# Keys and values of the memory between the steps of differential attention and gated memory, a choice from 100 pairs, 32 early keys, and other links around the routing

## The reference

```python
s_top, i_top = lax.top_k(s, K)                                     # K = 16, s: 128 keys
cand = s_top[:, :, 0, :, None] + s_top[:, :, 1, None, :]           # 256 sums per head
best, pos = lax.top_k(cand.reshape(T, PEER_HEADS, K * K), K)
...
a = jax.nn.gelu(jnp.einsum('thkd,td->thk', u, xb))                 # u = expert_u[ib]
out = jnp.einsum('thk,thkd->td', gb * a, expert_v[ib])
...
x = x + hybrid_mixer(rms_norm_2(x, norm_mix_g[l]), ...)            # differential attention, mLSTM
x = x + cross_attention(rms_norm_2(x, norm_x_g[l]), rms_norm_2(mem, norm_mem_g[l]), ...)
...
k = (mem_n @ wk); v = (mem_n @ wv)                                 # mem_n: 256 x 1024
```

## Time and profile before

| | us |
|---|---|
| median of 3 runs | 3126.39 |
| lowest, highest | 3126.13, 3129.74 |
| the profiled execution, its own time | 3126.0 |
| its span, first to last instruction | 3124.3 |
| busy: PE, DVE, ACT, POOL | 2733.4, 2077.2, 1336.7, 742.3 |
| mean granted clock of PE, share of 2.4 GHz | 0.935 |

### The profile page before, as it was taken

One profiled execution on the slowest core, in us unless ns is written; L12 is line 12 of the kernel. 1 busy time (PEld: TensorE's weight loads), 2 busy tenths in 40 slices (PEclk: granted clock), 3 DMA queues, 4 the chain that ended last, 5 costly groups with the idle time before them and its releaser, 6 DMA issues. The chain is left out here.

```text
span 3124.3 us, 35863 instructions
## 1 busy us (share of the span) xinstructions
PE 2733.4 (87%) x12788; PEld 2212.3 (71%) x12788; DVE 2077.2 (66%) x3565; ACT 1336.7 (43%) x2049; POOL 742.3 (24%) x562
## 2 busy tenths in 40 slices
PE   4976879799969999999999995895589699999994
PEld 3434668566757999999999994663367588888883
DVE  4334547799957777777777775415633489989984
ACT  2112552115643333333333334225333278878873
POOL 1000023141023333334334331430121221122220
PEclk8978989899989999999999997997789799999997
DMA  7710011333579988888888872220022399999993
GB/s 251 242 58 17 1 56 58 115 118 126 211 284 315 312 288 289 288 288 288 300 295 291 298 248 61 83 80 32 2 82 62 148 319 394 374 374 372 365 361 129
DMA packets 261487, 646.34 MB, mean 207 GB/s; under 512 B 47836, under 2 KB 104924, under 8 KB 260060
## 3 DMA queue, kind: packets, MB, share of 16 engines
q1 hardware_dynamic: 214892, 501.88, 44.8%
q0 software_dynamic: 46448, 142.67, 13.8%
HBM read 614.47 MB, written 55.12 MB: 214 GB/s over the span
## 5 line engine op out<-in xcount | busy, mean ns | idle before, releaser
L2826 ACT ACTIVATE ex_w_hi<-expert_raw 128x1024 fp32r<-128x1024 f32 x384 | 376.9, 1074 | 49.4 <-DMA expert_raw<-in_w 26.8
L1710 PE MATMUL bank<-v_hi,peer_w_hi 128*128 128x512 f32 x768 | 301.1, 392 | 21.5 <-DVE peer_w_lo L1816 21.5
L212 POOL TENSOR_TENSOR w_lo<-ring,w_hi 128x512 fp32r<-128x512 f32 (+1 forms) x136 | 173.3, 1306 | 557.3 <-ACT w_hi L202 557.3
L2872 DVE TENSOR_TENSOR ex_w_lo<-expert_raw,ex_w_hi 128x1024 fp32r<-128x1024 f32 x256 | 296.7, 1219 | 9.5 <-ACT ex_w_hi L2826 8.0
L1710 PE MATMUL bank<-v_hi,peer_w_lo 128*128 128x512 f32 x768 | 301.3, 392 | 0.0
L1710 PE MATMUL bank<-v_lo,peer_w_hi 128*128 128x512 f32 x768 | 301.2, 392 | 0.0
L1752 ACT ACTIVATE v_hi<-v_in 128x1024 fp32r<-128x1024 f32 x128 | 129.7, 1054 | 349.1 <-PE bank L1710 327.6
L1698 PE MATMUL bank<-h_hi,u_lo 128*128 128x384 f32 x832 | 278.6, 335 | 0.0
L1698 PE MATMUL bank<-h_hi,u_hi 128*128 128x384 f32 x832 | 278.5, 335 | 0.0
L1698 PE MATMUL bank<-h_lo,u_hi 128*128 128x384 f32 x832 | 278.3, 334 | 0.0
L1685 POOL DMA_INDIRECT got_rows<-in_u_rows,diff x128 | 186.2, 1455 | 311.9 <-DVE got_rows L1784 283.7
(11 more groups left out here) (495 smaller groups left out, 6201.2 us busy)
## 6 DMA issues: line engine op xcount, KB each, us to landing
expert_raw<-in_w SPq DMA_DIRECT2D x384, 512.0 KB, 9.2
v_in<-in_expert_v SPq DMA_DIRECT2D x128, 512.0 KB
u_in<-in_u_tiles SPq DMA_DIRECT2D x104, 512.0 KB
ada_in<-in_w_ada SPq DMA_DIRECT2D x48, 512.0 KB, 5.2
gates_by_key<-spread SPq DMA_DIRECT2D x6, 4096.0 KB, 11.5
gate_in<-gates_by_key SPq DMA_DIRECT2D x384, 64.0 KB
ring<-in_w_in SPq DMA_DIRECT2D x11, 2048.0 KB, 8.4
early_u<-in_u_tiles SPq DMA_DIRECT2D x24, 512.0 KB, 3.8
```

The source lines that it names most:

```text
L212: eng.tensor_tensor(g.w_lo[:, k, 0:cols], g.ring[u % RING][:, k, 0:cols], g.w_hi[:, k, 0:cols].bitcast(F32), ALU.subtract).then_inc(s["z_f ...
L1710: last = pe.matmul(g.bank[2 + o][:, :], x[:, par, e, i * P:(i + 1) * P], v[:, par, e, c], start=(first and n == 0), stop=(final and n == 3 ...
L2826: act.activation(hi[kind][:, c, :], raw_piece(raw, u * PIECES + c), ACT.Copy).then_inc(s["r_hi"], 1)
L2872: dve.tensor_tensor(lo[which][:, c, :], raw_piece(raw, u * PIECES + c), hi[which][:, c, :].bitcast(F32), ALU.subtract).then_inc(s["r_lo"], 1)
```

## The change

1. **Memory.** Class `MemoryRows` keeps normalising and turning in `choose_experts` and stores the result `mem_t` (1 MB) in DRAM. A new class `Memory` makes keys and values in 16 groups of 256 columns. A group is made in two halves, `part`, of four 128x256 matmuls each, in one bank (7); the next group's first part waits until ACT has copied the bank out. Ten parts stand in `differential`, one after each unit from u = 6; four stand at the head of PE's queue in `mlstm`, and 18 between its score products. Sums in `differential` then use one bank instead of two, so that each waits for ACT's copy of the one before. The weight units of the memory (19 to 22) come between those of `w_in_2` and `w_out_2`, and the loads ahead are moved with them.
2. **Choice.** `top16` runs over 100 sums instead of 256 (the 3 best first keys with all 16 second ones, the other 13 with 4). POOL adds 384 + 416 elements per token tile instead of 2048; DVE has one cast and four small operations more for the ranks.
3. **Early keys.** `EARLY_CHOOSING` is 20 instead of 12, so EQ is 16 instead of 12 and HALFWAY 38 instead of 36; after it a step gathers 128/26 = 4.92 rows. The statistics of the memory go on ACT's queue behind the second gelu instead of the fourth.
4. **Routing.** SP clears `lists` ahead of the 12 loads; the first two row gathers are issued by POOL inside `route`, as soon as `first_slots` is there; the wait for the last scatter goes from POOL's end of `run_experts` to SP in `finish`; the clearing of `moe_rows` goes into the guarded part of `run_overflow`; and the gain of `finish` is loaded first.

```diff
-EARLY_BEFORE, EARLY_CHOOSING, EARLY_SPREADING = 4, 12, 12
+EARLY_BEFORE, EARLY_CHOOSING, EARLY_SPREADING = 4, 20, 12
...
+    def part(self, pe, index):
+        j, half = index // 2, index % 2
+        n = self.groups[j]
+        u = self.first_unit + n // self.PER_UNIT
+        if half == 0:
+            g.weights(pe, u)
+            if j:
+                pe.wait_ge(s["q_out"], j)
+        w = g.ring[u % RING]
+        for k in range(half * self.HALF_K, (half + 1) * self.HALF_K):
+            ...
+            last = pe.matmul(self.slot(), x, y, start=(k == 0), stop=(k == DC - 1))
+        if half == 1:
+            last.then_inc(g.dense, 1)
...
@@ choose_experts
+LONG, SHORT = 3, 4
+PAIRS = LONG * TOPK + (TOPK - LONG) * SHORT
-                        top16(dve, count, s["h_dve"], [(sums[:, i % 2, h + j].rearrange("p a b -> p (a b)"), work[:, j, :],
+                        top16(dve, count, s["h_dve"], [(pairs[i % 2][:, h + j], work[:, j, :],
-                step(dve.tensor_scalar(rank_i[:, 1], place[:], 15, None, ALU.bitwise_and))
+                step(dve.tensor_scalar(rank_i[:, 1], place[:], 2, None, ALU.arith_shift_right))
                 step(dve.tensor_copy(rank[:], rank_i[:]))
+                step(dve.tensor_copy(place_f[:], place[:]))
+                step(dve.scalar_tensor_tensor(rank[:, 0], rank[:, 1], float(LONG - LONG * TOPK // SHORT), rank[:, 0], ALU.add, ALU.max))
+                step(dve.tensor_scalar(base[:], rank[:, 0], float(SHORT), float(LONG * (TOPK - SHORT)), ALU.mult, ALU.add))
+                step(dve.scalar_tensor_tensor(base[:], rank[:, 0], float(TOPK), base[:], ALU.mult, ALU.min))
+                step(dve.tensor_tensor(rank[:, 1], place_f[:], base[:], ALU.subtract))
@@ differential, PE
-                    if u >= 2:
-                        pe.wait_ge(s["m_y"], u - 1)
+                    if u:
+                        pe.wait_ge(s["m_y"], u)
+                    if u >= N - 2 * MEMORY_FIRST:
+                        mem.part(pe, u - (N - 2 * MEMORY_FIRST))
@@ mlstm, PE
+            BEFORE = 4
+            def parts_done(n):
+                return BEFORE + (PARTS - BEFORE) * (n + 1) // (ML_H * TT)
+                for index in range(BEFORE):
+                    mem.part(pe, index)
...
                         pe.matmul(g.bank[2 + n % 2][:, 0:T - j * P], kt[:, h, j * P:(j + 1) * P], qt[:, h, j * P:T], start=True, stop=True).then_inc(s["n_s"], 1)
+                        if j < TT - 1:
+                            for index in range(parts_done(n - 1), parts_done(n)):
+                                mem.part(pe, index)
@@ route
             def _(sp):
+                sp.wait_ge(s["q_zero"], 1)
+                sp.dma_start(table.rearrange("(r p) o -> r (p o)", p=P), zero[:, :]).then_inc(s["q_clear"], 16)
                 sp.wait_ge(g.rows_stored, 2 * TT * 16)
                 begin(sp)
-                sp.wait_ge(s["q_zero"], 1)
-                sp.dma_start(table.rearrange("(r p) o -> r (p o)", p=P), zero[:, :]).then_inc(s["q_clear"], 16)
                 sp.wait_ge(s["q_clear"], 16)
...
+                pool.wait_ge(g.rows_stored, 2 * TT * 16)
+                pool.wait_ge(s["q_first"], 1)
+                for n in range(2):
+                    gather_rows(pool, g, first_slots, x_rows, x_in, n)
@@ run_experts, POOL
-                for n in range(3):
-                    gather(n)
+                gather(2)
...
-                for par in range(2):
-                    pool.wait_ge(s[f"r_st{par}"], NE // 2 * 16)
@@ finish, SP
+                for par in range(2):
+                    sp.wait_ge(y_stored[par], NE // 2 * 16)
```

More of the change, by code:

```diff
@@ L1414, in _ @@
                 memory.sp_rows(sp)
-                for n in range(2, EARLY_BEFORE):
-                    early.load(sp, n)
-                    early.keep(sp, n - 2)
-                for n in range(EARLY_BEFORE, EARLY_BEFORE + 2):
-                    early.load(sp, n)
-                    early.keep(sp, n - 2)
-                memory.sp(sp)
-                for n in range(EARLY_BEFORE, EARLY_CHOOSING):
+                for n in range(EARLY_CHOOSING):
                     early.keep(sp, n)
@@ L1479, in _ @@
             def _(act):
-                for n in range(EARLY_BEFORE):
+                early.gelu(act, 0)
+                early.gelu(act, 1)
+                memory.act_stats(act)
+                for n in range(2, EARLY_BEFORE):
                     early.gelu(act, n)
                 memory.act(act)
-                act.wait_ge(s["h_shift"], 1)
-                act.activation(gate[:], gate[:], ACT.Exp).then_inc(s["h_exp"], 1)
                 for n in range(EARLY_BEFORE, EARLY_CHOOSING):
+                    if n == EARLY_CHOOSING // 2:
+                        act.wait_ge(s["h_shift"], 1)
+                        act.activation(gate[:], gate[:], ACT.Exp).then_inc(s["h_exp"], 1)
                     early.gelu(act, n)
@@ L1963, in _, with differential @@
                 dve.sem_inc(s["l_rot"], 1)
-def differential(g, tok):
+def differential(g, tok, memory, t, mem_t):
     nc, a = g.nc, g.a
@@ L1986, in differential @@
         ms, rms, rs = (sb(n, [P, TT * DA_H]) for n in ("da_ms", "da_rms", "da_rs"))
-        with stage(nc, "m_par m_dve m_lam m_lexp flipped flip_out m_s0 m_s1 m_max m_e0 m_e1 m_a m_t m_pt m_o m_y m_sq m_root m_gain") as (block, s):
+        with stage(nc, "m_par m_dve m_lam m_lexp flipped flip_out m_s0 m_s1 m_max m_e0 m_e1 m_a m_t m_pt m_o m_y m_sq m_root m_gain" + Memory.SEMS) as (block, s):
+            mem = memory(s, list(range(MEMORY_FIRST)))
             @block.sync
@@ L2282, in sums @@
                         pe.wait_ge(s["n_y"], 2 * (h - 1))
[L2283 to L2284 removed]
+                    for tiles in ((0, 1, 2), (3,)):
+                        if h and tiles == (3,):
+                            pe.wait_ge(s["n_y"], 2 * h)
+                        for i in tiles:
                             for j in range(i + 1):
[L2286 to L2287 removed]
+                                last = pe.matmul(sums_at(h, i, i + 1), sd[:, h % 2, j, (i - j) * P:(i - j + 1) * P], mv[:, j, h, :], start=(j == 0), stop=(j == i))
                         last.then_inc(s["n_o"], 1)
@@ L2377, with gather_rows, route @@
 RAW = 3
-def route(g, begin, table, slot, weight, first_slots, over):
+def gather_rows(pool, g, first_slots, x_rows, x_in, n):
+    rows = g.ht[:, 0:4, :].rearrange("p (b k) t -> p b (k t)", b=2)
+    pool.indirect_dma_start(out=rows[:, n % 2, :], out_offset=None, in_=x_rows,
+                            in_offset=bass.IndirectOffsetOnAxis(ap=first_slots[:, n:n + 1], axis=0),
+                            bounds_check=2 * T - 1, oob_is_err=False).then_inc(x_in[n % 2], 16)
+def route(g, begin, table, slot, weight, first_slots, over, x_rows, x_in):
     nc = g.nc
@@ L2940, in gather @@
         def gather(pool):
+            for par in range(2):
+                pool.wait_ge(y_stored[par], NE // 2 * 16)
+            pool.memset(m.rows[:, :, :], 0.0).then_inc(s["r_zero"], 1)
+            pool.wait_ge(s["r_zero"], 1)
             pool.sem_inc(s["r_go"], 1)
@@ L2992, in _, with finish @@
             guarded(dve, gates)
-def finish(g, weight, y_rows, out):
+def finish(g, weight, y_rows, out, y_stored):
     nc, a = g.nc, g.a
@@ L3084, in plan_weights @@
     g.plan(a["w_in_2"][0], W2_GATES, 2 * ML_H, 2)
+    for name in ("w_xk_2", "w_xv_2"):
+        for i in range(2):
+            g.plan(a[name][0], i * BANK, BANK, Memory.PER_UNIT)
     for i in range(2):
@@ L3105, in second_mixer, with memory @@
             project_second(g, tok, mv, conv, mi, mf, first_unit)
-            differential(g, tok)
-            mlstm(g, tok, mv, conv, mi, mf)
+            with ExitStack() as both:
+                t = both.enter_context(nc.sbuf_tensor("mem_in", [P, DC, MEM], F32))
+                piece = both.enter_context(nc.sbuf_tensor("mem_piece", [P, 2, MEM], F32))
+                def memory(s, groups):
+                    return Memory(g, s, t, piece, first_unit + 8, mem_kt, mem_v, groups)
+                differential(g, tok, memory, t, mem_t)
+                mlstm(g, tok, mv, conv, mi, mf, memory)
         def mixed(k):
```

201 lines of the change are left out of this document (122 added, 79 removed).

## The result

| | us |
|---|---|
| changed kernel, median of 6 runs (lowest, highest) | 3108.86 (3098.03, 3113.84) |
| kernel before, beside it, median of 6 runs | 3127.01 (3123.98, 3139.37) |
| ratio of the two, 95% interval | 0.9937 [0.9919, 0.9955] |
| span of the profiled execution, after and before | 3103.7, 3124.3 |

The change makes the kernel 0.6% faster, some 20 us. The forecast was 3101, with 3083 to 3116 as its range.

What follows compares the result with a forecast made beforehand. It took PE to bound the long stretches and chains over several engines the short stages between. −21.5 − 30.2 + 12 + 24 − 5.3 − 4.2 = −25.2 from 3126.0 gave 3100.8, as a median 3101 us; range 3083 to 3116.

Steps and rivals of the forecast that it cites:

- Choosing stage: Choosing stage: memory's products leave PE (−61.7), eight early tiles come (+41.3), DVE keeps up; −21.5 us, bounds −15 and −25.
- Expert loop: Expert loop: four steps change from full to early, −7.55 us each; −30.2 us, bounds −25 and −33.
- Rival B: Expert loop gives less, added early steps at 10.3 and late ones 0.2 more: −20 stays, 3111 us; chance 0.12.
- Differential attention and gated memory: Second mixer: memory parts partly fill idle PE; +12 us (bounds +6, +20) and +24 us (bounds +18, +32).
- the lower of my two cases: Head of gated memory: four parts take 6.9 us at full clock against a 10.5 us wait, costing 0, not 3.3.
- Rival A: Differential attention and gated memory: the memory's products hide in PE's idle time, without the +36, 3065 us; chance 0.07.
- Rival D: Both mixer stretches: PE runs at 1.2 GHz, a part costs 3.45 us; slower, +65, 3191 us; chance 0.04.
- rival E: Memory's weights, 2 MB a unit in a ring of two, arrive late between parts; 3117 us; chance 0.03.
- Routing: Routing: early clear and two gathers inside it bring the experts' first product earlier; −5.3 us, bounds −3 and −7.5.
- The end: End: SP itself waits for the last scatter and loads at about 3093.3; −4.2 us, bounds −3 and −5.

Runs made afterwards that it cites:

- e9: Kernel before with only the choice from 100 sums added; 3121.77 us, ratio 0.9986 to the kernel before.
- e2: Changed kernel choosing from all 256 sums again, rank operations kept; 3121.82 us, ratio 0.9998 to the kernel before.
- e10: Kernel before with only EARLY_CHOOSING raised from 12 to 20; 3131.63 us, ratio 1.0014 to the kernel before.
- e1: Changed kernel with EARLY_CHOOSING back at 12; 3133.6 us, ratio 1.0022 to the kernel before.
- e3: Changed kernel with most memory parts moved from among the scores to the tails of differential attention and gated memory; 3089.75 us, ratio 0.9903 to the kernel before.
- e4: Changed kernel with the 1 MB memory load issued only after the two parameter loads have landed; 3111.72 us, ratio 0.9956 to the kernel before.
- e5: Changed kernel with the first two row gathers back in run_experts, early clear kept; 3106.64 us, ratio 0.9961 to the kernel before.
- e7: Changed kernel without the stage run_overflow, whose body is not run on these inputs; 3103.55 us, ratio 0.9951 to the kernel before.
- e8: e3 with the edits of e4 and e5; 3091.98 us, ratio 0.9897 to the kernel before.

## Why the prediction was right, and where it was off

**Choosing stage: right** (-21.5; -20.9 measured). PE's last tile ended the stage, DVE 4 us before it. PE is held for 6.2 us by what stays of the memory (6.4 forecast), and a group of four takes 4.8 (4.7). Behind the last gelu the stage got 1.7 shorter and not 1.1: I had let DVE's rounds end beside PE's last tile, and they ended 3 us behind it. I named DVE's wait for the memory's root only as a bound; it is 9.9 us long, and 20.1 in e9, where ACT makes the root at its old place. Ten us more would have gone beyond the cover of 4. So by this estimate, which no run tests, moving the root (item 3) is a condition of this term that I had not named. That the parts need each other was in the sum, but not said; e2, e9 and e10 show it.

**Expert loop: right** (-30.2; -32.3, and -29.5 between e1 and the changed kernel). Over all twelve executions the loop took 957.2 to 960.0 with 12 early steps and 925.4 to 927.7 with 16. The added early steps took 8.7, and the late steps stayed at 16.54. DVE's share behind HALFWAY is 0.79 where I had added 2 points to 0.72, but PE stays full, so nothing follows from it. Rival B is out.

**Differential attention and gated memory: right** (+12 and +24, together 36; 38.9, and 35.6 to 38.9 over the seven executions that share their code). The windows grew by 12.3 and 26.8; of the second, 1.6 is the one part at low clock. The parts at the head cost nothing, as in the lower of my two cases: they ended 0.8 before the gate rows, though half of them ran at low clock. Rival A is out by these windows, and e3 shows where its idle time lay. Rival D is out, with clocks of 0.97. So is rival E: in its 256 products of the memory PE waited 4.1 us for ACT's copies and never for a weight buffer.

**Not foreseen: +2.4 at the start of differential attention.** I counted the 1 MB load of `mem_in` at nothing and named no work that it stands beside; it stands beside the two parameter loads that everything there waits for (e4).

**Routing: over-sized** (-5.3; -3.4 to the first product, -3.5 to the last result). The step that failed is that the two gathers "end the stage; the next begins at 2490.6": with indirect DMAs at its end, the stage ended 3.4 us after the second gather. I took 0.5. In e5, with the early clear and without these gathers, the first product came 5.4 earlier than in the kernel before: the early clear alone gives about what I had forecast for the two edits together.

**The end: over-sized** (-4.2; -1.6). The step that failed is that SP waits for the scatter "and loads at about 3093.3". I read POOL's wait of 8.86 as the scatter's landing; it lands 2.5 us behind its issue, and most of the wait was there in e7 with nobody waiting for the scatter.

The sum of the terms was -25.2. With the measured ones (-20.9, -32.3, +38.9, +2.4, -3.5, -1.6) it is -17.0, plus 0.1 in the pieces between. The median came out 18.2 lower than that of the kernel before beside it, and the ratio's interval is 14 to 25 us. So the forecast's 25.2 lies at the edge of what was measured: the three large terms were right in cause and size, and the gap comes from the three small ones, each 2 to 3 us too good. That the range held owes something to its width.

## What to carry to other kernels

Work that can be made anywhere belongs where its engine waits for another engine's tail, not between steps of the stage that it bounds: look at windows, not at the busy share of a stage. There it was free or nearly so (0 and 2 us for the two tails of e3), as long as its copies don't stand before what the tail waits for. It also kept TensorE's clock up for the work behind: 1.00 in e3 and 0.94 in e8 for the scores, against 0.87. Where two engines end a stage together, a single edit shows little gain; judge such edits in pairs, and look for waits that shift when one of them gets faster. And a load that is early enough for its user can still be late for another's: issue the small loads that a stage starts with alone.

## What the runs showed of the hardware

A stage that ends with an indirect DMA on POOL ends late: 3.4 us after the second gather was issued in the changed kernel, 6.0 after the last scatter in e7, against 1.6 us from `first_slots` (1.1 of them DVE's own work) to the next stage in e5. The gathers' part of this is shown by e5, which differs from the changed kernel in them alone. The scatter had landed 2.5 us after its issue, so its landing doesn't explain 6.0; what else POOL or the end of the stage waits for is open.

TensorE's granted clock differs between executions of the same instructions, and single places cost 1 to 3 us by it: the first 10 us of `differential` (0.63 or 1.00) and the last expert (8.3 us from scatter to scatter at 1.00; 9.6, 11.0 and 11.1 where it fell).

The time of unchanged work moves from one execution to the next: the first early gelu came between 588.7 and 602.6 us. A difference below about 10 us between two profiled executions is read from pieces cut at the same instructions, not from the spans, and a piece of 100 to 200 us can itself be 3 to 5 us off (the mixers, spreading).
